# Half blocks of the sample state, prompt products inside the state loop, reading by scaled sums, outer product from PSUM

## What is computed

```python
def step(carry, inp):                       # for the samples: one token, L = 1
    C, n, m = carry
    ...
    s_inter = jnp.exp(m_inter - m_j)
    num = s_inter[..., None] * jnp.einsum('bhjd,bhde->bhje', qc, C) + jnp.einsum('bhjs,bhse->bhje', s, vc)
    den = s_inter * jnp.einsum('bhjd,bhd->bhj', qc, n) + s.sum(-1)
    hout = num / jnp.maximum(jnp.abs(den), jnp.exp(-m_j))[..., None]
    ...
    C_new = decay[..., None, None] * C + jnp.einsum('bhs,bhsd,bhse->bhde', wg, kc, vc)
    n_new = decay[..., None] * n + jnp.einsum('bhs,bhsd->bhd', wg, kc)
```

## Time and profile before

| what | value |
|---|---|
| median of 3 runs | 2730.23 us (2728.31 to 2730.34) |
| the profiled execution | 2729.83 us |
| its span in the profile | 2727.9 us |
| busy share of the span: PE, DVE, ACT, POOL | 91%, 65%, 56%, 14% |
| DMA over the span | 455.79 MB, mean 167 GB/s |
| DMA in the slices that hold the loop (from 1432 us, 68 us each) | 243, 352, 319, 267 GB/s |

### The profile page before, as it was taken

The page is one execution under the profiler, slowest core; times in us unless marked ns, Lnnn a source line. Parts: engine busy times, 40 slices in busy tenths (PEclk is TensorE's granted clock), DMA queues, the critical chain, the costliest instruction groups (busy, mean ns, idle before and its releaser), DMA issues. The chain is left out here.

```text
span 2727.9 us, 50270 instructions
## 1 busy us (share of the span) xinstructions
PE 2493.7 (91%) x17672; PEld 2204.7 (81%) x17672; DVE 1764.9 (65%) x3697; ACT 1516.0 (56%) x2992; POOL 377.0 (14%) x372
## 2 busy tenths in 40 slices
PE   6978999899978999997989998899999987999997
PEld 3658989888867999997665543798999986899997
DVE  6855698866697555557244446248886469655555
ACT  5644656576597555556413542255556569555554
POOL 0000344200052000000002111014440025000000
PEclk8989999999999999999989998999999999999999
DMA  6643444577502555443116987344444420344542
GB/s 232 255 141 138 156 154 160 183 260 261 200 0 75 176 180 185 180 175 130 50 38 243 352 319 267 116 163 154 170 169 165 176 106 0 135 175 183 184 175 103
DMA packets 65102, 455.79 MB, mean 167 GB/s; under 512 B 8656, under 2 KB 8864, under 8 KB 10224
## 3 DMA queue, kind: packets, MB, share of 16 engines
q1 hardware_dynamic: 52128, 379.61, 38.6%
q0 software_dynamic: 11120, 73.29, 7.0%
q10 hardware_dynamic: 1760, 1.68, 0.2%
HBM read 415.27 MB, written 39.27 MB: 167 GB/s over the span
## 5 line engine op out<-in xcount | busy, mean ns | idle before, releaser
L829 ACT ACTIVATE w_parts<-ring 128x512 fp32r<-128x512 f32 x1376 | 851.2, 630 | 846.7 <-PE ps L427 771.3
L1232 DVE TENSOR_TENSOR w_parts<-ring,w_parts 128x512 fp32r<-128x512 f32 x1232 | 853.6, 704 | 605.5 <-ACT w_parts L829 596.4
L427 PE MATMUL ps<-h_hi,w_parts 128*128 128x264 f32 x5376 | 1020.7, 288 | 84.4 <-DVE w_parts L1232 58.9
L427 PEld LDWEIGHTS ps<-h_hi,w_parts 128*128 128x128 f32 x5376 | 853.0, 191 | 124.1 <-issue 69.1
L427 PE MATMUL ps<-h_lo,w_parts 128*128 128x264 f32 x2688 | 769.3, 286 | 0.0
L427 PE MATMUL ps<-g_parts,w_parts 128*128 128x264 f32 x6144 | 748.5, 284 | 6.7 <-DVE g_parts L1532 6.7
L427 PEld LDWEIGHTS ps<-g_parts,w_parts 128*128 128x128 f32 x6144 | 748.1, 189 | 7.0 <-issue 7.0
L427 PEld LDWEIGHTS ps<-h_lo,w_parts 128*128 128x128 f32 x2688 | 514.3, 191 | 2.0
L1136 POOL TENSOR_TENSOR w_parts<-ring,w_parts 128x512 fp32r<-128x512 f32 x144 | 211.3, 1469 | 476.0 <-ACT w_parts L829 475.6
L829 ACT ACTIVATE SCR<-SCR 128x128 f32<-128x128 f32 (+3 forms) x540 | 212.7, 490 | 13.9 <-POOL SCR L1151 9.6
L427 PE MATMUL ps<-SCR 128*128 128x128 f32 x1056 | 156.2, 293 | 63.5 <-DVE SCR L1503 45.8
(11 more groups left out here) (178 smaller groups left out, 1513.8 us busy)
## 6 DMA issues: line engine op xcount, KB each, us to landing
ring<-in_stream SPq DMA_DIRECT2D x362, 1024.0 KB, 4.8
BIG<-in_C POOLq DMA_DIRECT2D x32, 1024.0 KB, 8.1
out_C_s<-BIG POOLq DMA_DIRECT2D x32, 1024.0 KB, 5.9
out_C_p<-BIG POOLq DMA_DIRECT2D x16, 256.0 KB, 2.3
x<-in_x ACTq DMA_DIRECT2D x1, 1056.0 KB, 15.0
out_y<-BIG POOLq DMA_DIRECT2D x1, 1056.0 KB, 4.2
consts<-in_consts ACTq DMA_DIRECT2D x1, 256.0 KB, 10.4
BIG<-in_gates POOLq DMA_DIRECT2D x1, 192.0 KB, 2.6
```

Source lines behind the costliest of these rows:

```text
L427: return nc.tensor.matmul(out, lhsT, rhs, start=start, stop=stop, skip_group_check=shared)
L829: return nc.scalar.activation(to, of, f, **kw_)
L1232: tt(w_lo[:, j % HALVES, :], half_of(n, half), w_hi[:, j % HALVES, :].bitcast(F32), ALU.subtract).then_inc(lo_ready[half], 1)
```

## The change

The state is now moved and updated in units of half a C (two chunks, 512 KB): 64 units, u = 2 m + q, in 8 buffers (4 MB in all, against 5 MB), which take the place of `qT` and `kT`; the samples' columns of these are copied out before, to `qs` and `kw`.

- POOL issues the first 8 loads behind `st_done` (before: one whole C there, four behind the last prompt product). In the loop it stores a unit as soon as it is updated (`C_new`, before: `C_read`), every fourth unit also a prompt chunk, and loads the unit five further on, once the unit three back has been summed (`rd_ready`) and its store has landed.
- ACT scales a unit by decay in place (`scale_C`, 128 x 1024, one turn ahead), scales its first chunk by q into `rd` (`scale_rd`, 128 x 512), and copies every second turn a prompt chunk from PSUM to `Cst` (two buffers, before eight). The four ACTIVATEs of the outer product are gone.
- DVE adds kw times the spread v, taken straight from PSUM, to each chunk (four instructions of 128 x 512 a turn, line 1645 gone), and adds the second chunk times q to `rd` (`sum_rd`, two of 128 x 512).
- PE spreads v with one fp32r matmul of 16 rows (v in a high and a low part: `v_stack`, built by ACT and DVE ahead of the loop), does a prompt product in every second turn, and reads a turn with two fp32 matmuls of a column of ones at the unit's row (`one_col`) against `rd`. The sums of all heads and samples stand in 32 rows of one bank: one copy and 4 transposes follow, for four copies and 16.
- The stage of the prompt products ahead of the loop is gone, and so is `qz`. ACT's first `high` waits for the numerators in its place.

The core of the diff:

```diff
-        Cbuf = [big(MB + 2 * MT, HC, MHD)] + [big(VB + i * HC * MHD, HC, MHD) for i in range(4)]
+        Cbuf = [big(MB + (1 + i // 4) * MT + i % 4 * 2 * MHD, 2, MHD) for i in range(8)]
 ...
+        UNITS = 2 * NSMP * HEADS
 ...
-            for n in range(KM):
+            def prompt_C(n):
                 hd = n // HC
-                if n >= 4:
-                    pe.wait_ge(cp_copied, n - 3)
+                if n >= 2:
+                    pe.wait_ge(cp_copied, n - 1)
 ...
+            def spread_v(m):
+                b, hd = m // HEADS, m % HEADS
+                if m >= 2:
+                    pe.wait_ge(C_new, 2 * (m - 2) + 2)
+                mm(ps[:, m % 2, :], v_pick[:, b:b + 1].to_broadcast([2 * NSMP, P]),
+                   v_stack[:, hd * MHD:(hd + 1) * MHD]).then_inc(vb_done, 1)
             def read_C(m):
 ...
-                pe.wait_ge(C_new, 2 * m + 2)
-                for c in range(HC):
-                    last = mm(ps[0:NSMP, 4 + hd, :], qz[:, hd * HC + c, b * NSMP:(b + 1) * NSMP],
-                              Cbuf[m % CBUFS][:, c, :], b == 0 and c == 0, b == NSMP - 1 and c == HC - 1)
-                last.then_inc(C_read, 1)
+                for q in range(2):
+                    pe.wait_ge(rd_ready, 2 * m + q + 1)
+                    last = mm(ps[0:HEADS * NSMP, 4, :], one_col[:, at:at + HEADS * NSMP], rd[:, q, :],
+                              m == 0 and q == 0, m == NSMP * HEADS - 1 and q == 1)
+                    last.then_inc(C_read, 1)
 ...
+            spread_v(0)
             for m in range(NSMP * HEADS):
+                if m + 1 < NSMP * HEADS:
+                    spread_v(m + 1)
                 if m < KM:
 ...
                     split_chunk(ps[:, 2 + m % 2, 0:TOK], n0 + m, HALF["ml_z"] + 2 * m)
+                if m >= 1:
+                    read_C(m - 1)
+                if m % 2 == 0:
+                    prompt_C(m // 2)
 ...
+                            func(v_stack[:, o], ps[0:2 * NSMP, n % 4, :], ACT.Copy,
+                                 scale=col("v_sign")[0:2 * NSMP]).then_inc(v_signed, 1)
+                            func(v_raw[0:2 * NSMP, o], ps[0:2 * NSMP, n % 4, :], ACT.Copy).then_inc(vk_copied, 1)
 ...
             act.wait_ge(sqn_ready, 1)
-            act.wait_ge(cp_copied, KM)
+            act.wait_ge(num_done, HEADS)
 ...
+            def scale_C(m):
+                for q in range(2):
+                    u = 2 * m + q
+                    act.wait_ge(C_in[u % CBUFS], 16 * (u // CBUFS + 1))
+                    func(C_u, C_u, ACT.Copy, scale=bc[:, hd, 0, b:b + 1]).then_inc(C_scaled, 1)
+            def scale_rd(m):
+                for q in range(2):
+                    u = 2 * m + q
+                    act.wait_ge(C_new, u + 1)
+                    if m >= 1:
+                        act.wait_ge(C_read, u - 1)
+                    func(rd[:, q, :], Cbuf[u % CBUFS][:, 0, :], ACT.Copy,
+                         scale=qs[:, hd * HC + 2 * q, b:b + 1]).then_inc(rd_scaled, 1)
 ...
-                    for i in range(HC // 2):
-                        c = q * (HC // 2) + i
-                        last = func(vk[q][:, i, :], ps[:, m % 2, :], ACT.Copy, scale=kw[:, hd * HC + c, b:b + 1])
-                    last.then_inc(vb_used, 1)
 ...
+                if m + 1 < NSMP * HEADS:
+                    scale_C(m + 1)
+                scale_rd(m)
+                if m % 2 == 0:
+                    n = m // 2
+                    act.wait_ge(cp_done, n + 1)
+                    if n >= 2:
+                        act.wait_ge(cp_stored[n % 2], 16 * (n // 2))
+                    func(Cst[:, n % 2, :], ps[:, 5 + n % 2, :], ACT.Copy).then_inc(cp_copied, 1)
 ...
+            pool.wait_ge(qs_ready, 2)
+            pool.wait_ge(st_done, 1)
+            for u in range(CBUFS):
+                load_C(u)
 ...
+            LAG = 3
+            for u in range(UNITS):
+                pool.wait_ge(C_new, u + 1)
+                pool.dma_start(half_C(C_s_o, u), flat(Cbuf[u % CBUFS])).then_inc(C_out[u % CBUFS], 16)
+                if u % 4 == 3:
+                    n = u // 4
+                    pool.wait_ge(cp_copied, n + 1)
+                    pool.dma_start(C_p_o[n], Cst[:, n % 2, :]).then_inc(cp_stored[n % 2], 16)
+                old = u - LAG
+                if old >= 0 and old + CBUFS < UNITS:
+                    pool.wait_ge(rd_ready, old + 1)
+                    pool.wait_ge(C_out[old % CBUFS], 16 * (old // CBUFS + 1))
+                    load_C(old + CBUFS)
 ...
+            def update_C(m):
+                dve.wait_ge(vb_done, m + 1)
+                for q in range(2):
+                    u = 2 * m + q
+                    dve.wait_ge(C_scaled, u + 1)
+                    for i in range(2):
+                        C_i = Cbuf[u % CBUFS][:, i, :]
+                        last = stt(C_i, ps[:, m % 2, :], kw[:, hd * HC + 2 * q + i, b:b + 1], C_i, ALU.mult, ALU.add)
+                    last.then_inc(C_new, 1)
+            def sum_rd(m):
+                for q in range(2):
+                    u = 2 * m + q
+                    dve.wait_ge(rd_scaled, u + 1)
+                    stt(rd[:, q, :], Cbuf[u % CBUFS][:, 1, :], qs[:, hd * HC + 2 * q + 1, b:b + 1], rd[:, q, :],
+                        ALU.mult, ALU.add).then_inc(rd_ready, 1)
             for m in range(NSMP * HEADS):
-                    stt(Cm, Cm, bc[:, hd, 0, b:b + 1], flat(vk[q]), ALU.mult, ALU.add).then_inc(C_new, 1)
+                update_C(m)
+                if m >= 1:
+                    sum_rd(m - 1)
```

More of the change, by code:

```diff
@@ L127, in decoder_step @@
         lam8 = sb("lam8", [P, NC])
-        BIG = sb("BIG", [P, KEYS * TOK])
+        v_pick = sb("v_pick", [2 * NSMP, NSMP], F32R)
+        V_AT = KM * (3 + NPR) + KM * 4 * NSMP + 4 * KM * TOK + 4 * M_INNER
+        with nc.sbuf_tensor("BIG", [P, KEYS * TOK], F32) as BIG:
+            pass
+        sb("below_v_stack", [P, V_AT])
+        v_stack = sb("v_stack", [2 * NSMP, M_INNER], F32R)
+        sb("above_v_stack", [P, KEYS * TOK - V_AT - M_INNER])
         with nc.sbuf_tensor("SCR", [P, 6144], F32) as SCR:
@@ L213, in decoder_step @@
         qn = big(GB, KM, NSMP)
-        qz = big(GB + 384, KM, NSMP * NSMP)
+        qs = big(GB + 128, KM, NSMP)
+        one_col = big(GB + 256, 2 * HEADS * NSMP - 1)
         em = big(0, HEADS, NPR)
@@ L312, in decoder_step @@
         cp_copied = sem("cp_copied")
-        cp_stored = [sem(f"cp_stored{i}") for i in range(8)]
+        cp_stored = [sem(f"cp_stored{i}") for i in range(2)]
         sbc_done = sem("sbc_done")
@@ L374, in C_uses @@
         def C_uses(i):
-            return len(range(i, NSMP * HEADS, CBUFS))
+            return len(range(i, UNITS, CBUFS))
         AT_MU, AT_CENTRE, AT_SQUARE, AT_VAR, AT_MS, AT_SQRT, AT_SCALE, AT_SKIP, AT_Z = \
@@ L803, in _ @@
             read_C(NSMP * HEADS - 1)
-            for hd in range(HEADS):
-                pe.wait_ge(Cq_copied, hd + 1)
-                for e in range(hd * HC, (hd + 1) * HC):
-                    last = nc.tensor.transpose(ps[:, 0, e * NSMP:(e + 1) * NSMP], Cq[0:NSMP, e * P:(e + 1) * P],
-                                               ident[0:NSMP, 0:NSMP])
+            pe.wait_ge(Cq_copied, 1)
+            for e in range(HC):
+                last = nc.tensor.transpose(ps[:, 0, e * HEADS * NSMP:(e + 1) * HEADS * NSMP],
+                                           Cq[0:HEADS * NSMP, e * P:(e + 1) * P],
+                                           ident[0:HEADS * NSMP, 0:HEADS * NSMP])
             last.then_inc(Cq_turned, 1)
@@ L1204, in _ @@
             pool.wait_ge(ml_conv_stored, 16 * 2)
-            for i in range(8):
-                pool.wait_ge(cp_stored[i], 16 * KM // 8)
+            for i in range(2):
+                pool.wait_ge(cp_stored[i], 16 * KM // 2)
             for i in range(CBUFS):
@@ L1572, in _ @@
             ts(srow[H_, 2, :], ms, -1.0, None, ALU.mult).then_inc(rows_ready, 1)
+            for q in range(KM // 4):
+                dve.wait_ge(v_signed, q + 1)
+                dve.wait_ge(vk_copied, VS_AT + q + 1)
+                vq = v_stack[:, q * BANK:(q + 1) * BANK]
+                stt(vq, v_raw[0:2 * NSMP, q * BANK:(q + 1) * BANK], col("v_low")[0:2 * NSMP], vq.bitcast(F32),
+                    ALU.mult, ALU.add).then_inc(v_stacked, 1)
             dve.wait_ge(bcast_done, 1)
@@ L1806 @@
         cols[:H, where[name][0]] = a[name][0]
+    cols[:2 * B, where["v_sign"][0]] = np.repeat([1.0, -1.0], B)
+    cols[:2 * B, where["v_low"][0]] = np.repeat([0.0, 1.0], B)
     cols[:H, where["ml_m0"][0]:where["ml_m0"][0] + B] = a["state_mlstm_m"][0].T
```

137 lines of the change are left out of this document (65 added, 72 removed).

## The result

| what | value |
|---|---|
| kernel before, beside it on the same chip | 2729.27 us median of 4 runs (2727.5 to 2730.34) |
| changed kernel | 2687.1 us median of 4 runs (2684.9 to 2689.4) |
| ratio | 0.9846, 95% interval 0.9829 to 0.9863 |
| span of its profiled execution | 2683.9 us |

The change saves 42.2 us; 48.6 were forecast, on the way to 2681 us. The sum was nearly right. Its terms were less so, and they made up for one another: that is what the rest of this text is about.

What follows compares the result with a forecast made beforehand. PE bounds the kernel, the DMA 10 to 15% below; the DMA bounds it afterwards. From 1429.5, 198 us of DMA, 6.2 of tail and 3 of bursts end the loop at 1637, 48.6 us earlier: 2681 us, range 2660 to 2714.

Steps and rivals of the forecast that it cites:

- Ahead of the loop, +1.5 us: Before the loop: ACT's double copies of the samples' v delay PE's scores by 1.5 us, bounds 0.6 and 2.4.
- The prompt's stage leaves the path: Between numerators and loop: the 37 us stage of prompt products goes, its work returning inside the loop as 16 chunks.
- PE's turn of 6.3 us with z: In the loop: PE needs 6.3 us a turn with z and 3.2 without, against 7.7 and 4.6 before.
- The rate of 365 GB/s: Loop's DMA: share 0.96 of 380 GB/s gives 365, bounds 345 and 386.
- the 198 of the sum: Loop until the last load lands: 72.4 MB at 365 GB/s take 198 us, bounds 188 and 210.
- DVE's bursts, 3 us with bounds 0 and 8: Turns 18 to 29: DVE's prompt work leaves the DMA short now and then, costing 3 us, bounds 0 and 8.
- The tail of 6.2 us: Behind the last load's landing: scale, update, sum, read, copy, transposes and hand-overs take 6.2 us.
- The DMA's share at 0.83 (first): Loop: compute in bursts keeps the DMA at share 0.83, 315 GB/s, 230 us; time 2710 us; chance 0.15.
- More from the DMA (third): Loop: DMA gives 395 GB/s without bursts, 183 us; time 2663 us; chance 0.07 for below 2664.
- The clock (second): Loop's second half: PE's clock falls to 1.2 GHz, 130 us in place of 98; 2713 us; chance 0.08; sign: below 0.9.
- Halves that pay twice (fourth): Loop's loads and stores: half units pay the fixed time twice, 270 us at 1.8 under way; 2750 us; chance 0.05.
- Prompt products in the way (fifth): Loop's first half: prompt products delay PE's even turns (8.6 us, odd 5.2), ACT waits; 2700 us; chance 0.05.

## Why the prediction was right, and where it was not

**Ahead of the loop, +1.5 us: smaller, and the start came out for another reason.** Counted from ACT's last copy of 128 x 512 before the samples' v (1370.25 before, 1369.77 now), PE's scores begin 5.3 us on in place of 4.2, and the denominators end 53.9 us on in place of 53.5: of 1.1 us, 0.5 is left. The first update starts at 1427.05, where the forecast had the first spread and z chunk at 1426.5. What it waits for is DVE's own work, the four `low` of the first two weight tiles, which the forecast did not count on the path:

```profile
1424.55 2.50 DVE L1294 TENSOR_TENSOR w_parts<-ring,w_parts 128x512 fp32r<-128x512 f32 x4
```

The first store leaves at 1428.66; 1428.5 was forecast, and that is luck.

**The prompt's stage leaves the path: held.** Put back, it costs 36 us and relieves the loop of 11 to 12. The forecast's price for the way back was the stores' 3.7 MB among the 72.4, 10 us at its rate.

**PE's turn of 6.3 us with z: held as a size, not as a place.** PE's own pace is 13.08 / 2 = 6.5 us. The forecast put the DMA's turn at about 7 us, let the bound pass from PE to the DMA, and had PE wait. At 417 GB/s the 2.75 MB of a turn need 6.6 us, the two coincide, and in the changed kernel PE still waits for nothing while z is formed.

**The rate of 365 GB/s: right as a mean, by luck.** From 1429.5 to 1629 the row above reads a share of 0.96 and 364 GB/s, the forecast's two factors. But it is no one rate: 417 GB/s at 1.02 while z is formed, 386 at 1.00 behind that, 282 at 0.84 from 1580 on. The step that failed is the single price of a full share, 379 and 380 GB/s, got by dividing mean rates by mean shares, and with it the upper bound of 386: the sixty microseconds at 417 ran above it. The 415 of one ten-microsecond stretch in the earlier trace rows showed already that 386 was no ceiling, and it had rows of 8 KB. At 417 the 72.4 MB need 173.6 us, 24 fewer than the 198 of the sum. A rule of the Trainium skill that was weighed, 1 MiB or more in each DMA ("DMA: Bandwidth & Descriptors", "Rules for kernel authors"), is not borne out here: 0.5 MB in each move ran at 417 GB/s, with several under way, and 1 MB in each is no faster.

**DVE's bursts, 3 us with bounds 0 and 8: mis-sized.** Without them the time is 17 us less; with their work in a better row, the reciprocals on ACT and the last readings on PE, 15 us less. The step that failed set 26 + 12 x 4.0 = 74 us of DVE against 12 x 6.1 = 73 of DMA and called it even. The passes take 28.5 us of DVE in the changed kernel and a turn 4.1; the DMA's turn without z is 2.23 MB / 417 = 5.3 us. The twelve turns are 78 against 64, and the surplus stands on the path. This could have been read before: the 172 us of PE in the earlier trace rows end at 1634.2, and from 1635.6 to 1665.6 the chain of the kernel before runs over DVE, update and passes in turn (L1665 are the reciprocals, L1671 the skip passes):

```profile
1646.14 3.27 DVE BIG L1665
...
1654.56 2.87 DVE BIG L1671 x7
```

**How they cancel.** Against 417 GB/s, 1429.5 to 1462 is short of (417 - 346) x 32.5 = 2.3 MB or 5.5 us, 1462 to 1530 (414 GB/s) of 0.5 us, 1530 to 1580 of 3.7 us, 1580 to 1629 of (417 - 282) x 49 = 6.6 MB or 15.9 us. 173.6 + 5.5 + 0.5 + 3.7 + 15.9 = 199 us: the 198 of the sum, made of other parts. Why the first of these stretches falls short, at a share of 0.92, is not shown. The last load is issued at 1621.5, and ACT scales what it brings from 1629.2 on without having waited; 1627.5 was forecast.

**The tail of 6.2 us: mis-sized.** From there to 1639.9 it is some 11 us, since DVE and PE are still behind with turn 30; with the 3 us for the bursts the forecast had 9.2.

**The rivals.** The DMA's share at 0.83 (first) came true in the last quarter of the loop only, for the reason it named. More from the DMA (third) was right in the rate, 417 over its 395, and wrong in the time, since it came with "no bursts". The clock (second): the granted clock of the last stretch of the earlier trace rows is now 0.85, and 0.80 from 1580 to 1632, under the 0.9 that the text had set as the sign, and still not the cause of the loss: it cost about 1 us at the one place shown above, and that rival had 32 us. The sign was badly chosen, since it read 0.74 to 0.76 here in stretches where PE was busy 3.7 to 7.4 of 10 us and DVE 9.9. Halves that pay twice (fourth): whole blocks take the same time. Prompt products in the way (fifth): with the stage put back the turn gains 0.21 us and not a product's 0.95. The 8.6 us of that rival's even turns are not the sum of PE's parts, 0.3 + 3.1 + 1.8 + 2.3 = 7.5; its 2700 us do not hang on it. ACT's waits in the turns with z are for loads (5.2 us from 1470 to 1523) and for PE's products (3.6), as fits two bounds at one place.

## What to carry to other kernels

A total that comes out does not show that its terms are right: cut the stage at the point where the bound changes hands, and give each piece its own rate. Where two engines end a turn together, take away a piece of each alone and then both; either alone looks like no bound at all. Then look at an instruction that comes once a turn on the busiest engine: if its spacing stays the same when another engine's load is cut, that engine sets the pace, whatever the other's share says. When transfers bind a loop, what counts is the row of the bursts beside it: spread them, move work to the engine that has room in those turns, and leave a turn between a producer and an in-order engine that waits for it.
